# Query tiles of each attention head in falling order, the sample's tile first; the last head's thirds split from last to first

## The reference, cut to what matters

```python
h = rmsnorm(x) @ w_in                      # 1056 x 1024 by 1024 x 5648, fp32
oa = softmax(q1 k1^T)v - lam*softmax(q2 k2^T)v      # 4 heads; prompt: block-causal, chunks of 64
ob = gated linear attention                # 4 heads
oa = rmsnorm(oa) * silu(gate_a);  ob = rmsnorm(ob) * silu(gate_b)
mixed = sigmoid(g_a) * (oa @ w_branch_a) + sigmoid(g_b) * (ob @ w_branch_b)
y = rmsnorm(x + mixed @ w_out)
```

## Time and profile before

| | us |
|---|---|
| median of 3 runs | 951.71 (951.21 to 952.03) |
| the profiled execution: its time | 950.71 |
| the profiled execution: its span | 948.9 |
| TensorE busy in the span | 913.2 (96%) |
| VectorE, ScalarE busy | 483.7, 361.1 |

### The profile page before, as it was taken

One profiled execution on the slowest core, in us unless ns is written; L12 is line 12 of the kernel. 1 busy time (PEld: TensorE's weight loads), 2 busy tenths in 40 slices (PEclk: granted clock), 3 DMA queues, 4 the chain that ended last, 5 costly groups with the idle time before them and its releaser, 6 DMA issues. The chain is left out here.

```text
span 948.9 us, 16606 instructions
## 1 busy us (share of the span) xinstructions
PE 913.2 (96%) x6657; PEld 831.7 (88%) x6657; DVE 483.7 (51%) x1092; ACT 361.1 (38%) x871; POOL 122.6 (13%) x210
## 2 busy tenths in 40 slices
PE   4999999999999999999999999999998999999997
PEld 3799999989999889999889899898997989988884
DVE  5523287741217766244653464456447676991223
ACT  6545354422335444144443344335335332430011
POOL 1001122210102222000000000000001103540000
PEclk9999999999999999999999999999999999999998
DMA  8012011213110203251132201221124225551222
GB/s 261 15 46 66 24 47 61 78 46 99 45 45 24 63 28 102 59 192 37 32 137 74 74 1 58 62 74 46 46 78 128 83 77 170 175 172 44 89 89 77
DMA packets 85837, 74.07 MB, mean 78 GB/s; under 512 B 4697, under 2 KB 78082, under 8 KB 85506
## 3 DMA queue, kind: packets, MB, share of 16 engines
q1 hardware_dynamic: 85762, 73.02, 25.3%
HBM read 53.29 MB, written 19.73 MB: 77 GB/s over the span
## 5 line engine op out<-in xcount | busy, mean ns | idle before, releaser
L1384 PE MATMUL proj_bank<-x_hi,w_hi 128*128 128x352 f32 x1056 | 350.5, 332 | 0.9 <-ACT feature_stage L867 0.9
L1386 PE MATMUL proj_bank<-x_hi,w_lo 128*128 128x352 f32 x1056 | 339.5, 322 | 0.0
L1385 PE MATMUL proj_bank<-x_lo,w_hi 128*128 128x352 f32 x1056 | 338.9, 321 | 0.0
L1384 PEld LDWEIGHTS proj_bank<-x_hi,w_hi 128*128 128x128 f32 x1056 | 198.5, 188 | 4.2 <-issue 1.5
L1385 PEld LDWEIGHTS proj_bank<-x_lo,w_hi 128*128 128x128 f32 x1056 | 199.0, 188 | 0.0
L1386 PEld LDWEIGHTS proj_bank<-x_hi,w_lo 128*128 128x128 f32 x1056 | 198.2, 188 | 0.0
L620 DVE TENSOR_TENSOR w_lo<-w_raw,w_hi 128x1024 fp32r<-128x1024 f32 x49 | 59.9, 1223 | 76.5 <-ACT w_hi L616 76.5
L977 ACT ACTIVATE probs<-score_banks,softmax_stats 128x128 f32<-128x128 f32 (+8 forms) x72 | 51.2, 712 | 77.9 <-DVE softmax_stats L1300 69.2
L1045 POOL TENSOR_TENSOR stats<-stats,minus_half 128x1 f32<-128x1 f32 (+1 forms) x36 | 22.3, 620 | 371.5 <-DVE stats L1333 371.5
L1030 POOL TENSOR_TENSOR decays<-log_decay 128x128 f32<-128x128 f32 (+1 forms) x122 | 47.8, 424 | 156.5 <-ACT log_decay L914 156.5
L616 ACT ACTIVATE w_hi<-w_raw 128x1024 fp32r<-128x1024 f32 (+1 forms) x53 | 55.1, 1040 | 15.6 <-PE proj_bank L1386 14.8
(11 more groups left out here) (180 smaller groups left out, 1402.1 us busy)
## 6 DMA issues: line engine op xcount, KB each, us to landing
w_raw<-in_w_in SPq DMA_DIRECT2D x44, 512.0 KB, 4.6
merge_tanh_scratch<-feature_stage SPq DMA_DIRECT2D x16, 528.0 KB, 3.0
feature_stage<-merge_tanh_scratch SPq DMA_DIRECT2D x10, 528.0 KB, 3.9
x_rows<-in_x_prompt SPq DMA_DIRECT2D x8, 512.0 KB, 6.7
w_raw<-in_w_out SPq DMA_DIRECT2D x8, 512.0 KB, 4.6
branch_out<-in_x_prompt SPq DMA_DIRECT2D x8, 512.0 KB, 3.6
out<-branch_out SPq DMA_DIRECT2D x8, 512.0 KB, 2.6
tokens_stage<-merge_tanh_scratch SPq DMA_DIRECT2D x6, 528.0 KB, 3.7
```

Source lines behind the costliest of these rows:

```text
L1384: nc.tensor.matmul(out, wh, xh, start=first, stop=False)
L1385: nc.tensor.matmul(out, wh, xl, start=False, stop=False)
L1386: return nc.tensor.matmul(out, wl, xh, start=False, stop=last)
```

## The change

The nine tiles of each head are taken in the order TT, 7, 6, 5, 4, 3, 2, 1, 0. `TILE` maps the position p in the head to the tile. Scores, turned weights and value products of a tile are the same instructions as before. `load` counts the tiles in the new order, and so the units are dealt out anew. The cached keys of a head are now turned before the head begins: for head 0 just ahead of the first step, for heads 1 to 3 in the step of position 5 of the head before. In head 3, the thirds of the output are split from the last to the first, and the first three aunits take the thirds in that order.

```diff
+TILE = [TT] + list(range(TT - 1, -1, -1))
...
+    def cache(h):
+        stages.append(("cache", h))
+        if h + 1 < H:
+            stages.append(("cload", h + 1))
...
         if n < 2:
             stages.append(("gN" if n == 0 else "gT", 1, NTT - 1))
+    cache(0)
     flush()
...
             unit(*u)
-            if n == 0 and now and now[1] == 1:
-                stages.append(("cache", now[0]))
-                if now[0] + 1 < H:
-                    stages.append(("cload", now[0] + 1))
+            if n == 0 and now and now[1] == 5 and now[0] + 1 < H:
+                cache(now[0] + 1)
         stages.extend(more)
-        if one and len(groups(len(key_tiles(one[1])))) == 2:
+        if one and len(groups(len(key_tiles(TILE[one[1]])))) == 2:
             stages.append(("aX",) + one + (1,))
...
-        return sum(w * len(key_tiles((s - n) % NTT)) for n, w in ((0, 2), (1, 1), (2, 2)))
+        return sum(w * len(key_tiles(TILE[(s - n) % NTT])) for n, w in ((0, 2), (1, 1), (2, 2)))
...
-    return [(h, 0, T, NTT) for h in range(H - 1)] + [(H - 1, TH * th, TH * (th + 1), -(-TH * (th + 1) // P)) for th in range(3)]
+    return [(h, 0, T, NTT) for h in range(H - 1)] + [(H - 1, TH * th, TH * (th + 1), NTT - TH * th // P) for th in (2, 1, 0)]
+
+def third(v):
+    return 2 - v if v < 3 else v % 3
...
-                    f, th = st[1], st[2]
-                    v = 3 * f + th
+                    f, v = st[1], 3 * st[1] + st[2]
+                    th = third(v)
...
-                            pe.wait_ge(s_al, k + 1 + (th if k == H - 1 else 0))
+                            pe.wait_ge(s_al, k + 1 + (v if k == H - 1 else 0))
...
-                        pe.wait_ge(s_mxl, 3 * k + 1 + min((P * i + n - 1) // TH, 2))
+                        pe.wait_ge(s_mxl, 3 * k + 1 + min((P * i + n - 1) // TH, 2) if k else 3)
```

More of the change, by code:

```diff
@@ L962, in _ @@
                 elif kind == "aS":
-                    h, i = st[1], st[2]
-                    s = NTT * h + i
+                    h, p = st[1], st[2]
+                    i = TILE[p]
+                    s = NTT * h + p
                     n, nk = ntok(i), cols_of(i)[1]
@@ L971, in _ @@
                         h2, i2 = divmod(s - 2, NTT)
-                        for q in range(len(groups(len(key_tiles(i2))))):
+                        for q in range(len(groups(len(key_tiles(TILE[i2]))))):
                             filled(act, ("aX", h2, i2, q))
@@ L981, in _ @@
                 elif kind == "aX":
-                    h, i, q = st[1], st[2], st[3]
-                    s = NTT * h + i
+                    h, p, q = st[1], st[2], st[3]
+                    i = TILE[p]
+                    s = NTT * h + p
                     n = ntok(i)
@@ L1081, in mixed_lo @@
             def mixed_lo(v):
-                f, th = divmod(v, 3)
+                f, th = v // 3, third(v)
                 cols = slice(TH * th, TH * (th + 1))
@@ L1282, in _ @@
                 elif kind == "aN":
-                    h, i = st[1], st[2]
-                    s, n = NTT * h + i, ntok(i)
+                    h, p = st[1], st[2]
+                    i = TILE[p]
+                    s, n = NTT * h + p, ntok(i)
                     dve.wait_ge(s_ors, s + 1)
@@ L1335, in _ @@
                 elif kind == "aO":
-                    h, i = st[1], st[2]
+                    h, p = st[1], st[2]
+                    i = TILE[p]
                     n = ntok(i)
                     filled(dve, st)
-                    if h == 0 and i == 0:
+                    if h == 0 and p == 0:
                         dve.wait_ge(s_obst, 16)
```

35 lines of the change are left out of this document (19 added, 16 removed).

## The result

The changed kernel took 959.95 us (median of 4 executions, 958.33 to 961.60), against 951.71 before: a ratio of 1.0086, 95% interval 1.0066 to 1.0105. It is slower, as forecast, but by 8.2 us instead of 4.6, and 0.75 us above the upper end of the range.

The account below looks back on a forecast made before the run. TensorE was taken to bound the kernel, busy 913.2 of 948.9 us, so only its waits could change. Added waits of 9.2 less 4.65 removed gave +4.6 us, forecast 956.3 us, range 952.3 to 959.2.

Parts of the forecast that it names:

- cover and chain: Cover: TensorE's work from aO until it wants combined weights; chain: VectorE's path to them; a longer chain means a wait.
- item 1: End of head 3, asplit 1: TensorE waits 2.2 us for tile 0's combined weights.
- item 2: Head 3, a step before its end, asplit 0: TensorE waits 1.5 us for combined weights.
- item 3: End of position 7's step in head 1, silu of head 2's gate: TensorE waits 2.0 us.
- item 4: Bsplit 2: TensorE's next bunit waits 0.9 us for the third that VectorE splits at the step's end.
- item 5: Turned cache keys: waits for ScalarE's eviction, 0.7 three times and 0.8 before head 0's first scores, 2.9 us together.
- Rival B: ScalarE evicts the cached keys in time, so the cache's 2.9 us of waits vanish: 953.4 us; chance 0.14.
- C: VectorE reaches silu, bsplit and asplits at step ends earlier, removing up to 6.6 us: 949.7 us; chance 0.08.
- D: Waits breed waits: twelve tight steps at positions 6 to 8 cost 0.25 us more each, +3.0: 959.3; chance 0.12.
- rival E: In the drain, TensorE's waits halve its clock to 1.2 GHz; two bunits take 3.3 us more: 959.6; chance 0.03.
- 4.65: Microseconds the change would remove: the attention's five listed TensorE waits, 5.0, less 0.35 kept for evicted turned weights.
- item 6: Small waits at positions 7 and 8 add 0.3 us; tile 7's earlier values save 0.6: net -0.3.

Follow-up runs that it names:

- Experiment 1: The changed kernel with throwaway matmuls filling TensorE's four longest waits for combined weights: 956.10 us, ratio 1.0043 against the kernel before.
- experiment 9: The kernel before, order untouched, with VectorE repeating a small reciprocal 14 times ahead of the combining at tile 3 of heads 0 to 2: 960.71 us.
- experiment 6: The changed kernel with all repairs together: cache keys between units, silu, asplits and weight splits later, a bunit ahead of turned weights in the drain: 946.84 us.
- experiment 4: The changed kernel with the cached keys turned between two units again: 955.39 us over 10 executions, ratio 1.0039 against the kernel before.
- experiment 2: The changed kernel with asplits 0 and 1 put ahead of their step's units instead of behind them: 957.33 us, ratio 1.0056 against the kernel before.
- experiments 2 to 5 and 9: Third: the changed kernel with the silu of head 2's gate half a unit later, 956.68 us. Fifth: the changed kernel again, 958.27 us.

## Why the prediction was wrong, point by point

**The direction and the mechanism were right.** TensorE wants the small tiles' weights sooner than VectorE has combined them, and each wait forecast by cover and chain came. In the order of the list: item 1 2.26 for 2.2; item 2 1.38 for 1.5; item 3 1.80 for 2.0; item 4 1.22 for 0.9; item 5 0.66 + 3 x 0.59 = 2.4 for 2.9. Together 9.1 for 9.5. Rival B is out, since the cache's waits came; so is C, since the waits of items 1 to 4 came whole, 6.7 us for 6.6. D is out as well: it wanted 3.0 us in a dozen small pieces, and the changed kernel has no idle time of TensorE between 400 and 862 us beyond the waits listed.

**The step that failed was leaving out the clock, rival E.** I gave the clock a chance of 0.03 and left it out of the sum and of the range, and wrote that TensorE's busy time should stay within 1 us. It grew by 5.0. The reason given, that the slices with waits of 1.0 us show the top digit, could not carry it: no wait of the old kernel's attention was as long as the forecast ones, and a digit for 24 us can't show a stretch of 3 us anyway. E's mechanism was right in kind, and its place too narrow. The clock fell behind three waits and not the drain's alone, and each time it was back after a little over 3 us: 1.7 us each, 5.1 in all, where I had two whole bunits at half the clock, 3.3. That E's 959.6 is so near the measured 959.95 is luck: one stretch at the wrong price. Experiment 1 takes the clock out and leaves +4.5 of the +8.2, experiment 9 makes it in the old order. In hindsight, two stretches of 1.7 behind the two longest waits forecast (2.2 and 2.0) would have made 959.7, between the medians measured, 958.27 and 959.95.

The Trainium skill (TensorE: Matmul & The Clock Gate, A second HAM failure mode) had the direction, that idle times between groups of matmuls throttle the clock. This case agrees: 0.50 granted from 582 to 585 us, behind a wait of 1.80.

**Waits that the forecast missed.** Three, 2.5 us together: 1.55 and 0.60 at positions 5 and 7 of head 3, and 0.32 at 617.07. The timeline of VectorE in the changed kernel shows the first:

```profile
743.13 1.23 DVE L630 TENSOR_TENSOR w_lo<-w_raw,w_hi 128x1024 fp32r<-128x1024 f32 x1 [1.03 <-ACT w_hi L626]
744.28 0.95 DVE L1276 SCALAR_TENSOR_TENSOR mix_b<-tokens_stage,proj_bank 128x352 f32<-128x352 f32 x2
745.14 0.35 DVE L1360 SCALAR_TENSOR_TENSOR branch_out<-turn_bank,branch_norm_gains,da_gate 128x128 f32<-128x128 f32 x1
...
745.90 0.75 DVE L1328 SCALAR_TENSOR_TENSOR probs<-probs,softmax_stats,probs 128x512 f32<-128x512 f32 x1
```

A split of a branch weight stands ahead of two bunit products, and these ahead of aO and the combining. It is the same fault as items 1 to 3, a long operation in front of a step's end. I looked only for those that `step` puts right behind the last unit, and the weight's split is put there by the bunit itself. In experiment 6, with that split one third later, the 1.55 became 0.68.

**What the change removed was more than 4.65.** All attention rows, 5.0 us, are gone; also the 0.5, of which I had kept 0.35. The listed waits between 400 us and the branch's end went from 8.2 to 15.6, by 7.4, while the total without the clock grew by 4.9. The other 2.5 us are gain that the forecast did not have, beyond the 0.3 net of its item 6. One us of them is idle time, mostly pieces under 0.15 that the list leaves out: 450.00 - 440.80 = 9.2 of which 8.2 are listed before, against 462.00 - 446.43 = 15.6 after, all listed. Windows of the kernel before, then of the changed one:

```profile
400.00:850.00 450.00, 440.80 (x2890) 406.05 (x2888) 259.74 (x632) 178.23 (x430) 51.39 (x47) 1.00 0.29 89
```

```profile
400.00:862.00 462.00, 446.43 (x2899) 412.60 (x2898) 261.42 (x635) 178.91 (x431) 51.20 (x47) 0.99 0.29 87
```

The remaining 1.5 I have not traced to rows. The forecast also took no account of a row in its own list: a bunit's wait of 0.7 at 723.82, inside the attention, for which the profile names no releaser ("issue"). In the changed kernel the one such wait has 1.03, at 793.74. So the sum of 4.6 was met partly by luck, because two errors cancelled: 2.5 of waits missed, and some 2.5 of gain missed. The worry that the branch products would take lateness back did not come true either; their own waits grew a little, for `mix_work` from 1.5 to 1.8.

**Not settled.** Why a wait is followed by a low stretch in one execution and not in the next. The 1.80 was so in three profiled executions and not in experiment 4's; the 1.9 in one of three places; a 1.81 for `w_lo` in experiment 2 and the 1.38 in none that was profiled. The 2.26 was so in all four profiled executions that had it, and the pair of 1.55 and 1.22 in all five. So the length of a wait alone doesn't decide it. The clock's part of the difference between the medians is therefore itself spread: the changed kernel's eight executions went from 956.07 to 961.60. The Trainium skill (TensorE: Matmul & The Clock Gate, What's actually happening) says that the chip's watch over TensorE's activity runs freely and doesn't start anew with the kernel, so that the moment at which the clock first rises differs from run to run. That this holds for waits in mid-kernel too would fit the ten executions of experiment 4, but the page doesn't say it, and no run here shows the watch itself.

## What to carry to other kernels

When a change puts waits of about 2 us into an engine that is otherwise full, price the clock behind them as well as the waits: here 1.7 us for each, about as much again, in some executions and not in others. The sum of the waits alone is then the lower end of the range. Before an order of steps is blamed or praised, list every operation over a microsecond that the program puts ahead of a step's end on the engine that TensorE waits for, whichever helper puts it there, and move these first: here that turned +7.3 us into -4.2, while the same edits did nothing in the old order. To learn what the clock costs, fill the waits with throwaway matmuls: it needs no other change, and here the spread between executions shrank with it, from 3.3 and 4.0 us to 1.3 in experiment 1.

## What the runs showed of the hardware

Waits of 1.8 to 2.3 us and a pair of 1.55 and 1.22 us, in an engine that otherwise stood hardly at all, were followed by 1.2 GHz for a little over 3 us, costing 1.7 us each time, the same wherever windows show it (experiments 2 to 5 and 9, and the changed kernel's own profile). It didn't come each time: from the same program, executions with mean clocks of 0.993 to 0.999 differed by up to 4.7 us (experiment 4). The spread of the times alone is a weak sign of it: the kernel before spread over 0.8 to 3.4 us in its sessions, the changed one over 3.3 and 4.0. The mean clock is a better one, once the part behind the last matmul, 0.001 to 0.003 of it, is allowed for.
